# One inverse per right-hand side: the chunked delta rule of a hybrid decoder layer

## The chip, the cores and the metric

The kernel runs on one core of a Trainium2 chip, as one launch. The metric is the device time of the launch in microseconds, the median over the timed runs. The engines are named as in the profile: PE (matmul), PEld (PE's weight loads, which overlap its matmuls), DVE (vector), ACT (scalar), POOL (GpSimd), SP (which issues the weight DMAs).

## What is computed

One decoder layer for 256 prompt tokens and 8 x 8 sample tokens, 320 columns in all: an input projection, three token mixers (RG-LRU, gated delta rule, causal pooling), their gated sum, an output projection and an MLP. The change is in the delta rule, for each of 8 heads:

```
a_mat = eye(C) + where(strict, beta[..., None] * decay * kk, 0.0)
eg = exp(gamma)
rhs = concatenate([beta[..., None] * v, (beta * eg)[..., None] * k], axis=-1)
sol = triangular_solve(a_mat, rhs, lower=True, unit_diagonal=True)
u_c, wk_c = sol[..., :DV], sol[..., DV:]
...
def step(s, inp):
    w = uc - einsum('bhck,bhkv->bhcv', wkc, s)
    o = einsum('bhck,bhkv->bhcv', qg_c, s) + einsum('bhij,bhjv->bhiv', qk_c, w)
    s = gl_c[..., None, None] * s + einsum('bhck,bhcv->bhkv', kd_c, w)
```

With X the inverse of a_mat, w = X (beta v) - X (beta e^gamma k) S, which is also X (beta v - beta e^gamma k S).

## The kernel before

Channels lie on partitions and the 320 tokens on columns. Nearly all work on PE is projections. Their weights stream in tiles of 512 x 256 (512 KB): SP loads a tile into a ring of six (`load`, L251), ACT rounds it to a high part (`split`, L662), DVE makes the low part (`split`, L936), and PE takes the tile in eight blocks of three matmuls, high by high, high by low, low by high (`tile`, L1607; `product`, L1601). PE frees the tile's slot when it is done.

The small work of the mixers is put by hand between these blocks. The delta rule's heads 0 to 3 run under the gated projection of the LRU branch (`gated`, 4 iterations of 12 tiles), heads 4 to 7 under that of the pooling branch. A head is cut into numbered steps k (`dn_step`, one function on each of PE, L1740, DVE, L1295, and ACT, L789; POOL's part is `head`, L482). `dn_place` (L634) says behind which tile and block PE does step k. The first head of each half (0 and 4) is "peeled": its steps lie closer together, since it begins in the middle of an iteration. DVE and ACT do step k some four tiles earlier in their own order of weight tiles (`dn_steps`, L646, and for the peeled heads the lists in `late`), so they stand and wait at each step until PE has come to it, and PE has four tiles in hand meanwhile.

The 256 prompt tokens are two chunks of 128; the 64 sample tokens, eight sequences of eight, are a third. The steps of a head:

- k = 0, 1: rows of decays are spread by PE, DVE scales keys and queries (KT, QT, and KB, the keys by beta), PE forms the products of keys with keys and queries, and turns values and keys over. ACT scales the turned ones into VB (values by beta), KBG (keys by beta and e^gamma) and KDC. POOL masks the decay and forms QG1 and half of WQS, the queries by e^gamma (L490, L491).
- k = 3 to 14: six levels that build XT, the transposed inverse, in PE and DVE by turns.
- k = 15: PE applies the inverse to VB (three products) and to KBG (two: 128 columns of the second chunk and 64 of the samples). ACT copies the five results out of PSUM: W0, U12 (two), the negated samples' half of WQS, and WK1.
- k = 16: PE multiplies W0, does eight narrow products (32 columns of WQS by each sequence's state), and forms the state after the first chunk; ACT copies it (S1), DVE copies the narrow ones (WS).
- k = 17: PE multiplies S1 with WK1 and picks rows of WS; DVE adds both to U12 and spreads the samples (WX).
- k = 18: outputs and new states.

An fp32 product in these steps shows as two matmul rows in the trace (a count of x10 is five products).

Of the kernel before, what the change touches and what calls it, by code (L numbers as in the profile page):

```python
# [6 lines left out]
ALU = mybir.AluOpType  # L7
# [84 lines left out]
def build(nc, A):  # L92
    with ExitStack() as ctx:
# [68 lines left out]
        XT, KT, QT, KB, EG, WK1, QG1, WQS, DTM, LT, QKD = (  # L162
# [3 lines left out]
        VB, KBG, KDC = scr(o, 3 * P), scr(o + 3 * P, 3 * P), scr(o + 6 * P, 3 * P)  # L166
# [29 lines left out]
        def sem(name):  # L196
# [26 lines left out]
         w1_psum, w_ready, fin_psum, dn_done, ss_loaded, ss_stored) = map(sem, (  # L223
# [3 lines left out]
            "dn_done", "dn_state_loaded", "dn_state_stored"))  # L227
# [102 lines left out]
        def _(pool):  # L330
# [151 lines left out]
            def head(h, following):  # L482
# [6 lines left out]
                pool.wait_ge(vt_ready, h + 1)  # L489
                pool.tensor_tensor(QG1, QT[:, P:2 * P], EG[:, P:2 * P], ALU.mult)  # L490
# [13 lines left out]
            def clear_rows():  # L504
# [5 lines left out]
                for t in (VB, KBG):  # L510
                    pool.memset(t[NS:P, 2 * P:3 * P], 0.0)
# [122 lines left out]
        def dn_place(k, peeled):  # L634


            if peeled:
                after = (0, 6, 6, 13, 16, 20, 23, 27, 29, 32, 34, 38, 40, 44, 46, 48, 51, 54, 59)[k]
                return 5 + after // 8, after % 8
# [4 lines left out]
            return (5 + (k - 6) // 2, (3, 7)[k % 2]) if k < 18 else (11, 6)  # L644

        def dn_steps(step, h, late):  # L646

            steps = {}
            for k in (0, 1, *range(3, 19)):
# [7 lines left out]
        def _(act):  # L657
# [131 lines left out]
            def dn_step(h, k):  # L789
# [7 lines left out]
                elif k == 1:  # L797
# [29 lines left out]
            def late(it, t0, h0):  # L827

                if it == 0:
                    return {3: [lambda: gate(0, 1, t0, 0)], 4: [lambda: dn_step(h0, 15), lambda: dn_step(h0, 16)]}  # L830
# [1161 lines left out]
```

## Time and profile before

| | us |
|---|---|
| median of 3 timed runs | 2078.09 (2077.95 to 2078.2) |
| profiled execution, span from first to last instruction | 2076.3 |
| PE busy | 2059.8 (99%) |
| DVE busy | 1205.9 (58%) |
| ACT busy | 775.4 (37%) |
| POOL busy | 215.1 (10%) |
| L1742, most of the delta rule's small products, busy | 83.9 |

The busy times are unions over the whole span, and the engines overlap. Idle time on an engine that is not waited for costs nothing, so the views to read here are the chain that ended last, what the weight loads of PE waited for, and the timeline around the steps.

### The profile page before, as it was taken

The numbers are of one execution on the slowest core, as the hardware profiler recorded it, in microseconds if no ns is written. First come the engines' busy times: TensorE is split into PE (matmuls) and PEld (weight loads), VectorE is DVE, ScalarE is ACT, GpSimd is POOL, SyncE is SP. The second block draws the span as 40 slices with busy tenths as digits, with TensorE's granted clock in tenths as the row PEclk, the third lists the DMA queues.
The fourth block names the chain that finished last, engine by engine and source line by source line (L and its number), as shares of the span: only waits on it lengthen the run. The fifth ranks groups of instructions, "written<-read, shape, count | busy, mean of one in ns | idle before, by whom it ended". The sixth has DMA issues, their size and how long they took to land.

```text
span 2076.3 us, 35424 instructions
## 1 busy us (share of the span) xinstructions
PE 2059.8 (99%) x15117; PEld 2022.1 (97%) x15117; DVE 1205.9 (58%) x2065; ACT 775.4 (37%) x974; POOL 215.1 (10%) x358
## 2 busy tenths in 40 slices
PE   9999999999999999999999999999999999999997
PEld 9999999999999999999999999999999999999997
DVE  7989787566576666655545544444444444444444
ACT  5434555233333233333334433334233333333342
POOL 7322011111241110200001000000000000000001
PEclk9999999999999999999999999999999999999998
DMA  7444454444544444464444445444444445454443
GB/s 245 148 142 142 144 164 124 134 142 136 164 146 130 136 135 132 142 203 151 147 151 152 145 150 153 152 145 150 152 153 145 150 152 153 146 149 152 149 149 108
DMA packets 295644, 309.48 MB, mean 149 GB/s; under 512 B 9713, under 2 KB 290417, under 8 KB 295233
## 3 DMA queue, kind: packets, MB, share of 16 engines
q1 hardware_dynamic: 291616, 291.54, 44.8%
q0 software_dynamic: 3584, 15.55, 2.6%
q8 instruction: 119, 1.95, 0.4%
q14 instruction: 37, 0.30, 0.1%
q10 hardware_dynamic: 288, 0.15, 0.0%
HBM read 298.83 MB, written 8.37 MB: 148 GB/s over the span
## 4 chain that ended last, share of the span: by engine, by line
PE 90%; DVE 6%; issue 1%; POOL 1%; DMA 1%; ACT 1%; SPq 0%; DVEq 0%; ACTq 0%; POOLq 0%
PE main L1603 29%; PE main L1605 28%; PE main L1604 28%; PE aux L1742 3%; DVE lo L940 2%; DVE scratch L947 2%; DVE scratch L940 1%; DMA raw<-in_w_in 1%; DVE scratch L944 0%; PE aux L1854 0%; PE aux L1720 0%; POOL qkv L335 0%; DVE qkv L947 0%; POOL qkv L388 0%; ACT hi L668 0%
## 5 line engine op out<-in xcount | busy, mean ns | idle before, releaser
L940 DVE TENSOR_TENSOR lo<-raw,hi 128x1024 fp32r<-128x1024 f32 x544 | 660.4, 1231 | 342.2 <-ACT hi L668 334.7
L1603 PE MATMUL main<-x_hi,hi 128*128 128x320 f32 x2688 | 839.7, 312 | 1.8 <-DVE x_lo L947 0.8
L1605 PE MATMUL main<-x_hi,lo 128*128 128x320 f32 x2688 | 830.5, 309 | 0.0
L1604 PE MATMUL main<-x_lo,hi 128*128 128x320 f32 x2688 | 830.4, 309 | 0.0
L668 ACT ACTIVATE hi<-raw 128x1024 fp32r<-128x1024 f32 x544 | 564.1, 1054 | 674.8 <-DMA raw<-in_w_up 221.5
L1603 PEld LDWEIGHTS main<-x_hi,hi 128*128 128x128 f32 x2688 | 504.7, 188 | 9.1 <-DVE lo L940 3.8
L1604 PEld LDWEIGHTS main<-x_lo,hi 128*128 128x128 f32 x2688 | 504.8, 188 | 0.7
L1605 PEld LDWEIGHTS main<-x_hi,lo 128*128 128x128 f32 x2688 | 504.5, 188 | 0.0
L1603 PE MATMUL main<-o_hi,hi 128*128 128x320 f32 x1408 | 441.4, 314 | 0.0
L1605 PE MATMUL main<-o_hi,lo 128*128 128x320 f32 x1408 | 435.0, 309 | 0.0
L1604 PE MATMUL main<-o_lo,hi 128*128 128x320 f32 x1408 | 435.0, 309 | 0.0
L1603 PEld LDWEIGHTS main<-o_hi,hi 128*128 128x128 f32 x1408 | 264.4, 188 | 5.8 <-issue 4.6
L1604 PEld LDWEIGHTS main<-o_lo,hi 128*128 128x128 f32 x1408 | 264.5, 188 | 0.0
L1605 PEld LDWEIGHTS main<-o_hi,lo 128*128 128x128 f32 x1408 | 264.3, 188 | 0.0
L940 DVE TENSOR_TENSOR qkv<-main,qkv 128x320 f32<-128x320 f32 x144 | 64.0, 486 | 201.9 <-PE main L1605 201.8
L589 POOL COPY qkv<-gate 128x640 f32<-128x640 f32 x1 | 0.7, 723 | 868.4 <-ACT gate L909 868.4
L1742 PE MATMUL aux<-scratch 32*32 32x32 f32 (+2 forms) x1536 | 83.9, 223 | 0.5 <-DVE scratch L1319 0.4
L1742 PEld LDWEIGHTS aux<-scratch 32*32 32x32 f32 (+2 forms) x1536 | 65.4, 127 | 15.9 <-issue 11.6
L1603 PE MATMUL main<-merged_hi,hi 128*128 128x320 f32 x256 | 79.1, 309 | 0.0
L1604 PE MATMUL main<-merged_lo,hi 128*128 128x320 f32 x256 | 79.1, 309 | 0.0
L1605 PE MATMUL main<-merged_hi,lo 128*128 128x320 f32 x256 | 79.1, 309 | 0.0
L940 DVE TENSOR_TENSOR o_lo<-scratch,o_hi 128x640 fp32r<-128x640 f32 x44 | 36.3, 826 | 59.3 <-ACT o_hi L900 50.4
(283 smaller groups left out, 1212.8 us busy)
## 6 DMA issues: line engine op xcount, KB each, us to landing
raw<-in_w_in SPq DMA_DIRECT2D x210, 512.0 KB, 3.5
raw<-in_w_up SPq DMA_DIRECT2D x128, 512.0 KB, 3.7
raw<-in_w_down SPq DMA_DIRECT2D x128, 512.0 KB, 3.3
raw<-in_w_back SPq DMA_DIRECT2D x80, 512.0 KB, 3.3
scratch<-in_s_in POOLq DMA_DIRECT2D x8, 512.0 KB, 4.9
out_s_out<-scratch POOLq DMA_DIRECT2D x8, 512.0 KB, 4.4
merged<-in_x SPq DMA_DIRECT2D x8, 320.0 KB, 7.6
qkv<-in_x POOLq DMA_DIRECT2D x1, 2560.0 KB, 10.2
```

The lines of the kernel that those rows point to most:

```text
L589: pool.tensor_copy(acc, GS[:]).then_inc(sq2_used, 1)
L668: act.activation(HI[:, slot * TILE:(slot + 1) * TILE], RAW[:, slot * TILE:(slot + 1) * TILE], ACT.Copy).then_inc(hi_ready, 1)
L940: return dve.tensor_tensor(out, a, b, op)
L947: return dve.scalar_tensor_tensor(out=out, in0=a, scalar=s, in1=b, op0=op0, op1=op1)
L1603: pe.matmul(bank, hi, xh, start=first, stop=False)
L1604: pe.matmul(bank, hi, xl, start=False, stop=False)
L1605: return pe.matmul(bank, lo, xh, start=False, stop=last)
L1742: return pe.matmul(out, a, b, start=True, stop=True)
```

## The change

The inverse is applied once, to the right-hand side less the keys' product with the state. POOL forms the scaled keys in the layout of channels on partitions (KG1 and the first half of WQS). KBG is gone. PE takes the state's products first, DVE subtracts them from VB in place, and PE applies the inverse to what is left. Step 15 is now X VB of the first chunk and the narrow products, 16 the state after the first chunk and the rows of WS, 17 the keys by S1 and the inverse for the samples, 18 (new) the inverse for the second chunk, 19 what was 18.

```diff
@@ def build(nc, A):
-        XT, KT, QT, KB, EG, WK1, QG1, WQS, DTM, LT, QKD = (
+        XT, KT, QT, KB, EG, KG1, QG1, WQS, DTM, LT, QKD = (
...
-        VB, KBG, KDC = scr(o, 3 * P), scr(o + 3 * P, 3 * P), scr(o + 6 * P, 3 * P)
+        VB, KDC = scr(o, 3 * P), scr(o + 6 * P, 3 * P)
@@ def head(h, following): and def clear_rows():
                 pool.wait_ge(vt_ready, h + 1)
+                pool.tensor_tensor(KG1, KB[:, P:2 * P], EG[:, P:2 * P], ALU.mult)
+                pool.tensor_tensor(samples_of(WQS, 0), samples_of(KB[:, NP:N], 0), samples_of(EG[:, NP:N], 0), ALU.mult)
                 pool.tensor_tensor(QG1, QT[:, P:2 * P], EG[:, P:2 * P], ALU.mult)
...
-                for t in (VB, KBG):
-                    pool.memset(t[NS:P, 2 * P:3 * P], 0.0)
+                pool.memset(VB[NS:P, 2 * P:3 * P], 0.0)
@@ def dn_place(k, peeled):
             if peeled:
-                after = (0, 6, 6, 13, 16, 20, 23, 27, 29, 32, 34, 38, 40, 44, 46, 48, 51, 54, 59)[k]
+                after = (0, 6, 6, 13, 16, 20, 23, 27, 29, 32, 34, 38, 40, 44, 46, 48, 51, 54, 58, 62)[k]
                 return 5 + after // 8, after % 8
...
-            return (5 + (k - 6) // 2, (3, 7)[k % 2]) if k < 18 else (11, 6)
+            return (5 + (k - 6) // 2, (3, 7)[k % 2])
@@ def _(act): def dn_step(h, k):
-                    for c, n in enumerate((P, P, NS)):
-                        act.activation(KBG[0:n, c * P:(c + 1) * P], AX[3][0:n, c * P:(c + 1) * P], ACT.Copy,
-                                       scale=cols(COL, h, 1, c * 56 + 48, 1, n))
...
                 elif k == 15:
                     act.wait_ge(uw_psum, h + 1)
-                    act.activation(W0, AX[0][:, 0:P], ACT.Copy)
-                    act.activation(U12[:, 0:P], AX[0][:, P:2 * P], ACT.Copy)
-                    act.activation(U12[0:NS, P:2 * P], AX[0][0:NS, 2 * P:3 * P], ACT.Copy)
-                    act.activation(samples_of(WQS, 0), samples_of(AX[1][:, NP:N], 0), ACT.Copy, scale=-1.0)
-                    act.activation(WK1, AX[1][:, P:2 * P], ACT.Copy, scale=-1.0).then_inc(w0_ready, 1)
+                    act.activation(W0, AX[0][:, 0:P], ACT.Copy).then_inc(w0_ready, 1)
                 elif k == 16:
...
+                elif k == 18:
+                    act.wait_ge(u1_psum, h + 1)
+                    act.activation(U12[:, 0:P], AX[2][:, P:2 * P], ACT.Copy).then_inc(u1_ready, 1)
@@ def _(dve): def dn_step(h, k):
+                elif k == 15:
+                    dve.wait_ge(uw_psum, h + 1)
+                    dve.tensor_copy(WS, AX[2][:, 2 * P:3 * P]).then_inc(ws_ready, 1)
                 elif k == 16:
                     dve.wait_ge(s1_psum, h + 1)
-                    dve.wait_ge(s1_ready, h + 1)
-                    dve.tensor_copy(WS, AX[2][:, 2 * P:3 * P]).then_inc(ws_ready, 1)
+                    tt(VB[0:NS, 2 * P:3 * P], VB[0:NS, 2 * P:3 * P], AX[1][0:NS, 2 * P:3 * P], ALU.subtract) \
+                        .then_inc(r2_ready, 1)
                 elif k == 17:
                     dve.wait_ge(w1_psum, h + 1)
-                    tt(U12[:, 0:P], U12[:, 0:P], AX[1][:, P:2 * P], ALU.add)
-                    link(tt(U12[0:NS, P:2 * P], U12[0:NS, P:2 * P], AX[1][0:NS, 2 * P:3 * P], ALU.add))
+                    tt(VB[:, P:2 * P], VB[:, P:2 * P], AX[1][:, P:2 * P], ALU.subtract).then_inc(r1_ready, 1)
+                    link(dve.tensor_copy(U12[0:NS, P:2 * P], AX[0][0:NS, 2 * P:3 * P]))
                     tt(WX.rearrange("p (b v) -> p b v", b=4), U12[0:NS, None, P:2 * P].to_broadcast([NS, 4, P]),
@@ def _(pe): def dn_step(h, k, first):
                 elif k == 15:
                     pe.wait_ge(x_ready, h * 7 + 7)
-                    for c in range(3):
-                        mm(AX[0][:, c * P:(c + 1) * P], wide_x[:, c * P:(c + 1) * P], VB[:, c * P:(c + 1) * P])
-                    for c, lo, hi in ((1, P, 2 * P), (2, NP, N)):
-                        ins = mm(AX[1][:, lo:hi], KBG[:, c * P:(c + 1) * P], XT[:, lo:hi])
+                    pe.wait_ge(qg_ready, h + 1)
+                    pe.wait_ge(ss_loaded, h * 16 + 16)
+                    mm(AX[0][:, 0:P], XT[:, 0:P], VB[:, 0:P])
+                    for r in range(2):
+                        for j in range(4):
+                            b = 2 * j + r
+                            ins = pe.matmul(AX[2][32 * j:32 * (j + 1), 2 * P:3 * P],
+                                            WQS[:, 32 * b - 16 * r:32 * b - 16 * r + 32], SS[:, b * P:(b + 1) * P],
+                                            start=r == 0, stop=r == 1)
                     ins.then_inc(uw_psum, 1)
                 elif k == 16:
                     pe.wait_ge(w0_ready, h + 1)
-                    pe.wait_ge(qg_ready, h + 1)
-                    pe.wait_ge(ss_loaded, h * 16 + 16)
-                    mm(AX[3][:, 0:P], W0, QKD[:, 0:P])
...
-                    mm(AX[2][:, 0:P], KDC[:, 0:P], W0).then_inc(s1_psum, 1)
+                    pe.wait_ge(ws_ready, h + 1)
+                    mm(AX[2][:, 0:P], KDC[:, 0:P], W0)
+                    mm(AX[1][:, 2 * P:3 * P], SELW[:], WS)
+                    mm(AX[3][:, 0:P], W0, QKD[:, 0:P]).then_inc(s1_psum, 1)
                 elif k == 17:
                     pe.wait_ge(s1_ready, h + 1)
-                    pe.wait_ge(ws_ready, h + 1)
-                    mm(AX[1][:, P:2 * P], WK1, S1)
-                    mm(AX[1][:, 2 * P:3 * P], SELW[:], WS).then_inc(w1_psum, 1)
+                    pe.wait_ge(r2_ready, h + 1)
+                    mm(AX[1][:, P:2 * P], KG1, S1)
+                    mm(AX[0][:, 2 * P:3 * P], wide_x[:, 2 * P:3 * P], VB[:, 2 * P:3 * P]).then_inc(w1_psum, 1)
                 elif k == 18:
+                    pe.wait_ge(r1_ready, h + 1)
+                    mm(AX[2][:, P:2 * P], XT[:, P:2 * P], VB[:, P:2 * P]).then_inc(u1_psum, 1)
+                elif k == 19:
                     pe.wait_ge(w_ready, h + 1)
+                    pe.wait_ge(u1_ready, h + 1)
```

The lists for the peeled heads get ACT's step 18 behind the same tile as DVE's step 17, and DVE's step 15 ahead of 16.

PE's instructions around step 15 of head 1, before (L1742 is the small products, aux the PSUM banks they go to, scratch the tiles of the delta rule):

```order
L1605 MATMUL main<-x_hi,lo 128x320
L1742 MATMUL aux<-scratch 128x128 [waits dn_x]
L1742 MATMUL aux<-scratch 128x128 x3
L1742 MATMUL aux<-scratch 128x64
L1603 MATMUL main<-o_hi,hi 128x320 [waits evacuated,lo_ready]
L1604 MATMUL main<-o_lo,hi 128x320
```

and now:

```order
L1606 MATMUL main<-x_hi,lo 128x320
L1743 MATMUL aux<-scratch 128x128 [waits dn_state_loaded,dn_qg,dn_x]
L1798 MATMUL aux<-scratch 32x128 x8
L1604 MATMUL main<-o_hi,hi 128x320 [waits evacuated,lo_ready]
L1605 MATMUL main<-o_lo,hi 128x320
```

Four full products leave step 15 (two of them for good), and the eight narrow ones come in from step 16, with their waits.

DVE's order in the same head, from the last level of the inverse to the copy of the outputs, before:

```order
L940 TENSOR_TENSOR scratch<-scratch,aux 128x256 [waits dn_z_psum]
L940 TENSOR_TENSOR lo<-raw,hi 128x1024 [waits hi_ready]
L1374 COPY scratch<-aux 128x128 [waits dn_s1,dn_s1_psum]
L940 TENSOR_TENSOR gate<-main,rms_scale 128x320 [waits evacuated,tile_used]
L940 TENSOR_TENSOR gate<-main,rms_scale 128x320
L940 TENSOR_TENSOR scratch<-scratch,aux 128x128 [waits dn_w1_psum]
L940 TENSOR_TENSOR scratch<-scratch,aux 64x128
L940 TENSOR_TENSOR scratch<-scratch,batch_mask 64x512 [waits dve_step]
L940 TENSOR_TENSOR lo<-raw,hi 128x1024 [waits hi_ready]
L1383 COPY qkv<-aux 128x320 [waits dn_fin_psum]
```

and now:

```order
L938 TENSOR_TENSOR scratch<-scratch,aux 128x256 [waits dn_z_psum]
L1371 COPY scratch<-aux 128x128 [waits dn_uw_psum]
L938 TENSOR_TENSOR lo<-raw,hi 128x1024 [waits hi_ready]
L938 TENSOR_TENSOR scratch<-scratch,aux 64x128 [waits dn_s1_psum]
L938 TENSOR_TENSOR gate<-main,rms_scale 128x320 [waits evacuated,tile_used]
L938 TENSOR_TENSOR gate<-main,rms_scale 128x320
L938 TENSOR_TENSOR scratch<-scratch,aux 128x128 [waits dn_w1_psum]
L1379 COPY scratch<-aux 64x128
L938 TENSOR_TENSOR scratch<-scratch,batch_mask 64x512 [waits dve_step]
L938 TENSOR_TENSOR lo<-raw,hi 128x1024 [waits hi_ready]
L1384 COPY qkv<-aux 128x320 [waits dn_fin_psum]
```

The copy WS moves ahead of a weight tile's split, the subtraction for the samples stands behind that split, and the one for the chunk behind the gate's two products.

## Rows read from the trace of the kernel before

**Rows 1.** The page's busy times, and one stretch of the view by stretches (PEclk is the last but two)

```profile
PE 2059.8 (99%) x15117; PEld 2022.1 (97%) x15117; DVE 1205.9 (58%) x2065; ACT 775.4 (37%) x974; POOL 215.1 (10%) x358
...
373.00:428.00 55.00, 55.00 (x516) 51.92 (x515) 33.68 (x83) 18.00 (x32) 7.84 (x11) 1.00 0.45 134
```

**Rows 2.** The page's chain that ended last, by line

```profile
PE main L1603 29%; PE main L1605 28%; PE main L1604 28%; PE aux L1742 3%; DVE lo L940 2%; DVE scratch L947 2%; DVE scratch L940 1%; DMA raw<-in_w_in 1%; DVE scratch L944 0%; PE aux L1854 0%; PE aux L1720 0%; POOL qkv L335 0%; DVE qkv L947 0%; POOL qkv L388 0%; ACT hi L668 0%
```

**Rows 3.** Waits of PE's weight loads: 326 to 368 us, 605 to 660, 660 to 820

```profile
PEld aux L1742 <- DVE scratch L940: 0.5, 2, 0.3
PEld aux L1742 <- DVE scratch L1319: 0.3, 1, 0.3
...
PEld aux L1742 <- DVE scratch L1319: 0.7, 1, 0.7
PEld aux L1742 <- DVE scratch L1353: 0.3, 1, 0.3
...
PEld aux L1742 <- DVE scratch L940: 0.6, 3, 0.2
```

**Rows 4.** Timeline of PE, head 1, steps 15 to 18 (start, duration, engine, line)

```profile
408.99 0.31 PE L1605 MATMUL main<-x_hi,lo 128*128 128x320 f32 x1
409.14 1.22 PE L1742 MATMUL aux<-scratch 128*128 128x128 f32 x10
...
410.40 0.31 PE L1604 MATMUL main<-o_lo,hi 128*128 128x320 f32 x1
...
411.87 0.31 PE L1605 MATMUL main<-o_hi,lo 128*128 128x320 f32 x1
...
413.38 0.31 PE L1604 MATMUL main<-o_lo,hi 128*128 128x320 f32 x1
...
414.85 0.31 PE L1605 MATMUL main<-o_hi,lo 128*128 128x320 f32 x1
...
415.59 0.31 PE L1604 MATMUL main<-o_lo,hi 128*128 128x320 f32 x1
...
418.96 0.33 PE L1816 MATMUL aux<-scratch 128*128 128x64 f32 x2
419.13 0.39 PE L1817 MATMUL aux<-ident,scratch 128*128 128x64 f32 x2
```

**Rows 5.** Timeline of ACT and DVE, head 1, steps 15 to 17

```profile
410.40 0.28 ACT L811 ACTIVATE scratch<-aux 128x128 f32<-128x128 f32 x1 [9.13 <-PE aux L1742]
...
411.15 1.06 ACT L668 ACTIVATE hi<-raw 128x1024 fp32r<-128x1024 f32 x1
...
412.25 1.23 DVE L940 TENSOR_TENSOR lo<-raw,hi 128x1024 fp32r<-128x1024 f32 x1 [4.24 <-ACT hi L668]
...
414.02 0.88 DVE L940 TENSOR_TENSOR gate<-main,rms_scale 128x320 f32<-128x320 f32 x2
415.64 0.48 DVE L940 TENSOR_TENSOR scratch<-scratch,aux 128x128 f32<-128x128 f32 x2 [0.74 <-PE aux L1742]
416.15 0.68 DVE L940 TENSOR_TENSOR scratch<-scratch,batch_mask 64x512 f32<-64x512 f32 x1
```

**Rows 6.** Timeline of DVE, head 0, steps 15 and 18

```profile
358.62 1.23 DVE L940 TENSOR_TENSOR lo<-raw,hi 128x1024 fp32r<-128x1024 f32 x1 [1.04 <-ACT hi L668]
...
368.24 2.40 DVE L947 SCALAR_TENSOR_TENSOR scratch<-scratch,aux 128x128 f32<-128x128 f32 x9
```

**Rows 7.** Timeline of POOL in head 0, DVE and PE in head 1, steps 1 and 3

```profile
331.67 1.44 POOL L490 TENSOR_TENSOR scratch<-scratch 128x128 f32<-128x128 f32 x1
333.08 1.30 POOL L491 TENSOR_TENSOR scratch<-scratch 128x64 f32<-128x64 f32 x1
...
376.90 1.53 DVE L940 TENSOR_TENSOR lo<-raw,hi 128x1024 fp32r<-128x1024 f32 x1 [0.91 <-ACT hi L668]
...
381.08 0.16 DVE L1319 STREAM_TRANSPOSE scratch<-scratch 64x32 f32<-64x32 f32 x1
...
383.45 0.38 PE L1742 MATMUL aux<-scratch 32*32 32x32 f32 x20
```

More of the change, by code:

```diff
@@ L226, in build @@
             "dn_z_psum", "dn_uw_psum", "dn_w0", "dn_s1_psum", "dn_s1", "dn_ws", "dn_w1_psum", "dn_w", "dn_fin_psum",
-            "dn_done", "dn_state_loaded", "dn_state_stored"))
+            "dn_done", "dn_state_loaded", "dn_state_stored", "dn_rhs_samples", "dn_rhs", "dn_u1_psum", "dn_u1"))
         pool_loaded, pfx_ready, ptail_copied, d_ready, py_psum = map(sem, (
@@ L643, in dn_place @@
                 return (5 + (k - 6) // 2, (2, 6)[k % 2])
-            return (5 + (k - 6) // 2, (3, 7)[k % 2]) if k < 18 else (11, 6)
+            return (5 + (k - 6) // 2, (3, 7)[k % 2])
         def dn_steps(step, h, late):
             steps = {}
-            for k in (0, 1, *range(3, 19)):
+            for k in (0, 1, *range(3, 20)):
                 pos = dn_place(k, False)[0] + 4
@@ L829, in late @@
                 if it == 0:
-                    return {3: [lambda: gate(0, 1, t0, 0)], 4: [lambda: dn_step(h0, 15), lambda: dn_step(h0, 16)]}
+                    return {3: [lambda: gate(0, 1, t0, 0)], 4: [lambda: dn_step(h0, 15), lambda: dn_step(h0, 16)],
+                            5: [lambda: dn_step(h0, 18)]}
                 steps = dn_steps(dn_step, it + h0, True)
@@ L1393, in gated @@
                 gate0, merge0 = lambda: gate(n0, t0, it, 0), lambda: merge(n0, t0, g0, it, 0, branch)
-                dn = [lambda k=k: dn_step(h0, k) for k in range(19)]
+                dn = [lambda k=k: dn_step(h0, k) for k in range(20)]
                 own = {8: [gate0], 10: [merge0]}
@@ L1404, in late @@
                 gate1, merge1 = lambda: gate(n0, t0, it, 1), lambda: merge(n0, t0, g0, it, 1, branch)
-                dn = [lambda k=k: dn_step(h0, k) for k in range(19)]
+                dn = [lambda k=k: dn_step(h0, k) for k in range(20)]
                 if h0 is not None and it == 0:
                     return {1: [dn[7], dn[8]], 2: [dn[9], dn[10], dn[11]], 3: [dn[12], gate1, dn[13], dn[14]],
-                            4: [dn[16]], 5: [dn[17], merge1, dn[18]]}
+                            4: [dn[15], dn[16]], 5: [dn[17], merge1, dn[19]]}
                 if h0 is None:
@@ L1797, in dn_step @@
                     pe.wait_ge(w0_ready, h + 1)
-                    pe.wait_ge(qg_ready, h + 1)
-                    pe.wait_ge(ss_loaded, h * 16 + 16)
-                    mm(AX[3][:, 0:P], W0, QKD[:, 0:P])
-                    for r in range(2):
-                        for j in range(4):
-                            b = 2 * j + r
-                            pe.matmul(AX[2][32 * j:32 * (j + 1), 2 * P:3 * P], WQS[:, 32 * b - 16 * r:32 * b - 16 * r + 32],
-                                      SS[:, b * P:(b + 1) * P], start=r == 0, stop=r == 1)
-                    mm(AX[2][:, 0:P], KDC[:, 0:P], W0).then_inc(s1_psum, 1)
+                    pe.wait_ge(ws_ready, h + 1)
+                    mm(AX[2][:, 0:P], KDC[:, 0:P], W0)
+                    mm(AX[1][:, 2 * P:3 * P], SELW[:], WS)
+                    mm(AX[3][:, 0:P], W0, QKD[:, 0:P]).then_inc(s1_psum, 1)
                 elif k == 17:
                     pe.wait_ge(s1_ready, h + 1)
-                    pe.wait_ge(ws_ready, h + 1)
-                    mm(AX[1][:, P:2 * P], WK1, S1)
-                    mm(AX[1][:, 2 * P:3 * P], SELW[:], WS).then_inc(w1_psum, 1)
+                    pe.wait_ge(r2_ready, h + 1)
+                    mm(AX[1][:, P:2 * P], KG1, S1)
+                    mm(AX[0][:, 2 * P:3 * P], wide_x[:, 2 * P:3 * P], VB[:, 2 * P:3 * P]).then_inc(w1_psum, 1)
                 elif k == 18:
+                    pe.wait_ge(r1_ready, h + 1)
+                    mm(AX[2][:, P:2 * P], XT[:, P:2 * P], VB[:, P:2 * P]).then_inc(u1_psum, 1)
+                elif k == 19:
                     pe.wait_ge(w_ready, h + 1)
+                    pe.wait_ge(u1_ready, h + 1)
                     pe.matmul(AX[3][:, P:2 * P], S1, QG1, start=True, stop=False)
@@ L1827, in gated @@
                     for h in (h0, it + h0) if it == 1 else (it + h0,):
-                        for k in (0, 1, *range(3, 19)):
+                        for k in (0, 1, *range(3, 20)):
                             j, b = dn_place(k, h == h0)
```

3 lines of the change are left out of this document (1 added, 2 removed).

## The prediction

> **What bounds the kernel now.** I read the page first for the busiest engine. PE is busy 99% of the span, and in the stretch from 373 to 428 us, which holds one whole head of the delta rule, PE is busy 55.00 of 55.00 us at a granted clock of 1.00 [rows 1]: the upper level, 2.4 GHz. The chain of waits says the same: 85% of it are the three lines of the large products and 3% is L1742, the small products of the delta rule [rows 2]. Last I read what PE's weight loads waited for. From 660 to 820 us (heads 5 to 7) there are three waits on DVE, 0.6 us together; head 4 has single waits of 0.7 and 0.3 us, head 0 has 0.5 and 0.3 [rows 3]. So what a head does on PE is paid in full, and what it does on DVE, ACT and POOL costs nothing until PE reaches a step whose input is not there. I therefore count PE's instructions, and then look for each new input whether it is in time.
>
> **The unit prices on PE** are in the timeline of head 1 [rows 4]. A large product starts 0.147 us after the one before it (from 410.40 to 411.87, ten of them). The cost of a step between two large ones is the time from the last large product before it to the second behind it, less two such pitches (the second, because the first is also stretched):
> - two products of 128 columns: 415.59 - 414.85 - 0.294 = 0.446 us, 0.223 each;
> - step 15, four of 128 columns and one of 64: 410.40 - 408.99 - 0.294 = 1.116 us, five times 0.223. The 64 columns cost as much as 128;
> - step 16, two of 128 and the eight narrow ones with the states: 413.38 - 411.87 - 0.294 = 1.216 us.
> A step as such has no price of its own here: five products in one step cost what they would in two.
>
> **The sum on PE, per head.** Removed: both products of the scaled keys with the inverse, one of 128 and one of 64 columns, 2 x 0.223 = 0.446 us. All others stay and are only dealt out otherwise: the eight narrow ones move from step 16 to 15, W0's with QKD goes behind two others in 16, the samples' product with the inverse moves from 15 to 17, that of the second chunk to the new step 18. Before: 1.116 + 1.216 + 0.446 = 2.778 us. Now: step 15 is 1.216 - 0.223 = 0.993, step 16 is 0.669, 17 is 0.446, 18 is 0.223, together 2.331. The difference is again 0.446 us, and 8 heads make **3.57 us**. The bounds: inside step 19 (old 18) a product of 64 columns is followed after 0.17 us [rows 4]. With 0.17 for the short one the sum is 8 x 0.39 = 3.1 us. I take 0.223, since in step 15 itself, where the product is removed, it cost that. The upper bound is 3.57 plus waits that PE has now.
>
> Each of these products is two matmul rows, so a row's pitch is 0.111 us. The Trainium skill (TensorE: Matmul & The Clock Gate, Back-to-back issue gap) gives about 81 ns for a matmul of 128 columns in a stream with its weight loads. By it the four rows that go are worth at most 8 x 4 x 0.081 = 2.6 us. The trace's pitch is a third above that figure, and the sum goes by the trace.
>
> **What leaves and joins the other engines.** ACT loses three scalings at step 1 and four of five copies at step 15, and gains one copy at step 18. POOL gains two products per head, ahead of the two it has. DVE gains one small copy of 64 rows and a step 15 that waits for PE. None of this is on the path by itself; what counts is when PE's inputs come. POOL's memset that goes is hidden as it was.
>
> **New waits of PE, middle heads** [rows 5]. Steps 15 to 19 now lie four blocks apart, 12 x 0.147 = 1.76 us.
> - Step 15 ends at about 410.1. ACT's copy W0 takes 0.28, and DVE's copy WS of the same size I take as equal: both there at 410.5; PE asks at 411.9.
> - Behind W0 ACT splits a weight tile (1.06 us) and DVE follows (1.23): 410.5 + 1.06 + 1.23 = 412.8. Only then does DVE subtract the samples (0.25): 413.1. PE asks in step 17 at 414.3. Behind these two on DVE wait the gate's two products (0.88 together), done at about 414.
> - Step 17's result is there at 414.9; the subtraction of the chunk takes 0.25, so 415.2; PE asks in step 18 at 416.5. The copy and the 0.68 us product behind it end at 416.2.
> - Step 18's result is copied by ACT by 417.1; PE asks at 418.5.
> The least slack is 1.2 us. Step 19 stays within a block of where it was, and DVE's long update behind it with it.
>
> **New waits, heads 0 and 4** [rows 6]. Here the spacing is three blocks, 1.32 us, from 15 to 17. In head 0 DVE's split of 358.62 ends at 359.85, and WS is copied behind it: 360.15. PE wants it at 360.0: **0.2 us of waiting**. For the chunk's subtraction the chain is S1's copy until 361.5, ACT's split until 362.6, DVE's split of 1.23 until 363.8, the subtraction until 364.05; PE asks for it at 364.4, slack 0.35. Step 19 comes 1.0 us later than step 18 did, and the next head's first products wait for DVE's update behind it (the nine operations of 2.40 us, ended at 370.64 before): ready at about 371.8, asked for at 372.9. That is what is late next, if anything is.
>
> **The forecast**: 3.57 - 0.2 = 3.4 us less. On the profiled execution, 2076.3 to 2072.9 us of span. The timed runs have a median of 2078.09, 1.8 us above this span for what lies outside it; I take that as unchanged: 2078.09 - 3.4 = **2074.7 us**. 0.2% is 4.16 us, about what a measurement here can tell from no change, so this lies within it, if not by much (0.16%).
>
> **The rivals.**
> - **POOL holds DVE back at step 1.** The two new products come before the query's, so POOL reads SBUF for longer while DVE builds the blocks whose inverse PE waits for in step 3. Their prices are those of the two that exist, 1.44 and up to 1.30 us [rows 7]. In head 1 the blocks are ready at 381.24 and PE comes at 383.45: 2.2 us of cover against 1.44 + 0.32. In heads 0 and 4 PE waits at that step already [rows 3], so there any delay is paid: at most 2.74 + 1.76 = 4.5 us, giving 2074.7 + 4.5 = 2079.2 us; half of it 2077. Against it: most of DVE's step 1 already runs beside work of POOL. The Trainium skill (SBUF — State Buffer, SBUF: two separate sides) has it that a DVE operation with two SBUF inputs and a GpSimd operation exclude each other for the whole instruction; by that rule this rival would be the outcome. No row here shows a full block: DVE's split takes 1.53 us beside POOL's product [rows 7] and 1.23 alone [rows 5].
> - **The round trip that was added is too long: slower.** Step 17's subtraction stands on DVE behind a split, which needs a tile from DMA and ACT. Were that tile late in every head, PE would wait in step 17 or 18. It decides from 3.4 + 4.16 = 7.6 us, 0.95 us in each of 8 heads, that is an input 2.2 us later than worked out above for the middle heads. With 3 us the waiting is 1.8 us a head: 2074.7 + 14 = 2089 us. Against it: the tile that ACT splits at 411.15 needed no wait of its own, its idle time lies before the copy of 410.40.
> - **The waits that PE has now shrink too: faster.** ACT is free about 0.8 us sooner at step 1 (three operations of 0.28) and 0.5 sooner at step 15 (from 410.40 to 411.15, less one copy). If half of the 1.8 us of rows 3 that PE waits in heads 0 and 4 went, 3.57 + 0.9 gives 2073.6 us. Against it: those waits are on DVE's own results [rows 3], which ACT doesn't feed.
> - **The short product costs less than a full one.** Then the removal is worth 3.1 us, by the 0.17 us of rows 4, and the time is 2075.2 us.
>
> **Chances.** Forecast as told 0.75; POOL's hold 0.10; waits shrink 0.08; the short product 0.04; round trip 0.03. Faster by over 0.2% (under 2073.9): the third with a little of the forecast's spread, 0.11. Slower (over 2082.2): round trip and a rest of POOL's hold, 0.04. Within: 0.85. The range takes in the forecast's bounds (3.1 to 4.4 us) and half of POOL's hold: 2073.7 to 2077.2.
>
> **What would show it.** Right: 30 matmul rows a head in steps 15 to 18 instead of 34, 16 of them the narrow ones; those steps cost 2.33 us by the same reading; PE's waits on DVE grow by 0.2 in head 0 alone; ACT's nine scalings become six. Wrong: a new wait of PE on DVE's subtraction or ACT's U12 copy in heads 1 to 3 and 5 to 7; a longer wait at step 3 with POOL's products beside it (POOL's hold); a pitch other than 0.22 us for plain products, or a price for leaving the narrow ones towards a large product that no row of step 16 has, where a plain product follows them.

## The result and the profile after

The change makes the kernel slower. The median of 11 runs is 2083.03 us (2081.24 to 2085.28) against 2078.03 us for the kernel before on the same chip (2077.41 to 2078.95); the ratio is 1.0024, 95% interval 1.0017 to 1.0032. The forecast was 2074.7 us. The profiled execution has a span of 2081.1 us against 2076.3: 4.8 us more. One of the eleven runs of pool_twice below had a mean granted clock of 0.849 and took 2216.06 us; it is in the range given there and not in the ratio.

The page of the changed kernel, and its chain that ended last by line. Against [rows 1] PE has 32 matmul rows fewer (15085 for 15117), ACT 48 instructions fewer, POOL 14 and DVE 8 more; one entry of the chain has no counterpart in [rows 2], `DMA out_p_out<-scratch`, the store of the prompt's state:

```profile
PE 2059.1 (99%) x15085; PEld 2020.7 (97%) x15085; DVE 1208.4 (58%) x2073; ACT 766.3 (37%) x926; POOL 218.6 (11%) x372
...
PE main L1604 28%; PE main L1606 27%; PE main L1605 27%; PE aux L1743 3%; DVE lo L938 2%; DVE scratch L945 2%; DVE scratch L938 2%; DMA raw<-in_w_in 1%; DMA out_p_out<-scratch 1%; DVE scratch L942 0%; PE aux L1859 0%; PE aux L1721 0%; POOL qkv L335 0%; DVE qkv L945 0%; ACT hi L669 0%
```

The removed products are gone at the price that was forecast. The timeline of PE in head 1, steps 15 and 16, read as [rows 4] were (last large product before the step, second one behind it, less 0.294 us):

```profile
412.83 0.31 PE L1606 MATMUL main<-x_hi,lo 128*128 128x320 f32 x1
412.98 0.38 PE L1743 MATMUL aux<-scratch 128*128 128x128 f32 x2
413.30 0.64 PE L1798 MATMUL aux<-scratch 128*32 128x128 f32 x16
414.12 0.31 PE L1605 MATMUL main<-o_lo,hi 128*128 128x320 f32 x1
...
415.59 0.31 PE L1606 MATMUL main<-o_hi,lo 128*128 128x320 f32 x1
...
416.55 0.31 PE L1605 MATMUL main<-o_lo,hi 128*128 128x320 f32 x1
```

414.12 - 412.83 - 0.294 = 0.996 us, then 0.666, and read the same way 0.436 and 0.226 for steps 17 and 18: 2.32 us, where the steps cost 2.778 before and 2.331 were forecast. In no head does PE wait at step 17, 18 or 19.

The loss lies elsewhere. The waits of PE's weight loads in the changed kernel, from 368 to 422 us (head 1); the same rows with the same numbers stand from 660 to 715 us (head 5). Columns are total us, number, and us of the longest:

```profile
PEld aux L1743 <- DVE scratch L938: 2.1, 1, 2.1
...
PEld aux L1743 <- DVE scratch L1317: 0.8, 1, 0.8
```

L938 is step 4 and L1317 step 3. Before, head 5 had no wait over 0.2 us [rows 3]. And behind the second of these waits, in both heads, TensorE's granted clock falls to its lower level. Stretches of the view by stretches, the changed kernel (busy us and count of PE, PEld, DVE, ACT and POOL, then PEclk, share and GB/s of DMA):

```profile
384.00:387.90 3.90, 2.06 (x49) 1.75 (x49) 3.60 (x8) 0.50 (x1) 0.01 (x1) 1.00 0.39 125
387.90:391.30 3.40, 3.40 (x45) 2.96 (x33) 0.72 (x5) 2.13 (x3) 0.00 (x0) 0.52 0.02 5
391.30:395.00 3.70, 3.70 (x41) 3.28 (x41) 2.10 (x7) 0.94 (x1) 0.00 (x0) 0.98 0.43 142
677.90:681.50 3.60, 3.60 (x34) 3.21 (x33) 1.59 (x5) 1.42 (x2) 0.00 (x0) 0.53 0.27 91
```

For 3.4 us from 387.9 and 3.6 us from 677.9 the granted clock is 0.52 and 0.53 of 2.4 GHz: 1.2 GHz for nearly all of it. The kernel before has 1.00 in the same stretches. So PE did 3.40 x 0.48 = 1.6 us less work there than its busy time tells, and "PE busy 99%" shows nothing of it.

**Where 4.8 us come from.** The first small product of a head (step 0, four rows of `aux<-head_rows`) marks its start. Timeline of PE, the kernel before, then the changed one:

```profile
373.09 0.75 PE L1742 MATMUL aux<-head_rows,row_pickers 128*128 128x320 f32 x4
...
428.37 0.60 PE L1742 MATMUL aux<-head_rows,row_pickers 128*128 128x320 f32 x3
...
660.24 0.75 PE L1742 MATMUL aux<-head_rows,row_pickers 128*128 128x320 f32 x4
...
715.51 0.75 PE L1742 MATMUL aux<-head_rows,row_pickers 128*128 128x320 f32 x4
```

```profile
372.94 0.75 PE L1743 MATMUL aux<-head_rows,row_pickers 128*128 128x320 f32 x4
...
431.75 0.75 PE L1743 MATMUL aux<-head_rows,row_pickers 128*128 128x320 f32 x4
...
662.20 0.75 PE L1743 MATMUL aux<-head_rows,row_pickers 128*128 128x320 f32 x4
...
721.07 0.75 PE L1743 MATMUL aux<-head_rows,row_pickers 128*128 128x320 f32 x4
```

Head 1 took 428.37 - 373.09 = 55.28 us and takes 58.81, 3.53 more. Head 5 took 55.27 and takes 58.87, 3.60 more. These two make +7.13 us. All the rest is 2.3 us shorter: six heads save 0.45 each, 2.7 us, and by the same reading of the steps small waits give back 1.1 of it (0.7 at step 4 in heads 2, 6 and 7; 0.7 in head 0, of which 0.5 at step 10; less 0.3 that head 4 no longer waits). The 0.7 us that remain lie outside the steps of the delta rule. Within head 1 the sum closes: +3.53 and the 0.45 that was saved make 3.98. Steps 3, 4 and 5 cost 1.13, 2.58 and 0.96 us by the reading of [rows 4], where each cost 0.50 before: 3.17 of it. The other 0.8 lies in large products at the lower clock. By cause it is 1.6 us of clock and 2.4 us of waiting.

### The profile page after: what moved, and what is told of

It is laid out like the page before. It is cut to its first block, busy times and chain, and to the rows that moved or that the text cites. A ratio compares the mean times of both kernels' runs of the same rounds, so it can differ in the third digit from the quotient of the medians.

```text
span 2081.1 us, 35342 instructions
## 1 busy us (share of the span) xinstructions
PE 2059.1 (99%) x15085; PEld 2020.7 (97%) x15085; DVE 1208.4 (58%) x2073; ACT 766.3 (37%) x926; POOL 218.6 (11%) x372
## 4 chain that ended last, share of the span: by engine, by line
PE 87%; DVE 8%; DMA 2%; issue 1%; POOL 1%; ACT 1%; SPq 0%; DVEq 0%; ACTq 0%; POOLq 0%
PE main L1604 28%; PE main L1606 27%; PE main L1605 27%; PE aux L1743 3%; DVE lo L938 2%; DVE scratch L945 2%; DVE scratch L938 2%; DMA raw<-in_w_in 1%; DMA out_p_out<-scratch 1%; DVE scratch L942 0%; PE aux L1859 0%; PE aux L1721 0%; POOL qkv L335 0%; DVE qkv L945 0%; ACT hi L669 0%
## 5 line engine op out<-in xcount | busy, mean ns | idle before, releaser
L938 DVE TENSOR_TENSOR lo<-raw,hi 128x1024 fp32r<-128x1024 f32 x544 | 659.5, 1229 | 319.9 <-ACT hi L669 312.5
L938 DVE TENSOR_TENSOR qkv<-main,qkv 128x320 f32<-128x320 f32 x144 | 64.1, 486 | 202.8 <-PE main L1606 202.7
L938 DVE TENSOR_TENSOR o_lo<-scratch,o_hi 128x640 fp32r<-128x640 f32 x44 | 36.3, 825 | 59.3 <-ACT o_hi L898 50.4
```

Of the source, the lines that this page charges most:

```text
L938: return dve.tensor_tensor(out, a, b, op)
```

## How 1.2 us became 2.4

The chain does not run through PE. Timeline of POOL between heads 0 and 1, the kernel before: store of the samples' states, of the prompt's state (not shown), the load of the next head's states behind both, the masking of the decay behind the load's issue, and the first product behind the mask (start, duration; in brackets the idle time before and its releaser):

```profile
370.94 0.95 POOL L496 DMA_DIRECT2D out_s_out<-scratch  x1 [34.42 <-DVE scratch L947]
...
375.52 0.90 POOL L484 DMA_DIRECT2D scratch<-in_s_in  x1 [2.49 <-DMA out_p_out<-scratch]
376.44 0.88 POOL L487 TENSOR_TENSOR scratch<-scratch,mask_incl 128x320 f32<-128x320 f32 x1
377.27 1.48 POOL L490 TENSOR_TENSOR scratch<-scratch 128x128 f32<-128x128 f32 x1
```

The same of the changed kernel:

```profile
372.10 0.95 POOL L498 DMA_DIRECT2D out_s_out<-scratch  x1 [35.21 <-DVE scratch L945]
...
378.60 0.90 POOL L484 DMA_DIRECT2D scratch<-in_s_in  x1 [4.41 <-DMA out_p_out<-scratch]
379.52 0.89 POOL L487 TENSOR_TENSOR scratch<-scratch,mask_incl 128x320 f32<-128x320 f32 x1
380.36 0.47 POOL L490 TENSOR_TENSOR scratch<-scratch 128x128 f32<-128x128 f32 x1
```

The last step's update ends on DVE at 371.80 (its row is below), 1.16 us later than before, and the stores start 372.10 - 370.94 = 1.16 us later. They also take longer: from the first store to the release of the load it was 4.6 us and is 6.5. SP begins to issue the four weight tiles of this stretch at 369.76 before and at 369.62 now, so the later stores may fall behind more of the tiles' traffic, which no run separates; the 64 KB store lands 3.3 us after its issue before, and 5.3 now. The mask starts 3.08 us later. DVE, the changed kernel, head 0's last step and head 1's steps 1 to 4:

```profile
369.40 2.40 DVE L945 SCALAR_TENSOR_TENSOR scratch<-scratch,aux 128x128 f32<-128x128 f32 x9
...
376.75 1.23 DVE L938 TENSOR_TENSOR lo<-raw,hi 128x1024 fp32r<-128x1024 f32 x1 [0.92 <-ACT hi L669]
380.51 0.55 DVE L938 TENSOR_TENSOR scratch<-aux,scratch 128x256 f32<-128x256 f32 x2 [2.54 <-POOL scratch L487]
381.10 1.76 DVE L938 TENSOR_TENSOR scratch<-scratch,block_masks 32x96 f32<-32x96 f32 x4
...
383.70 0.16 DVE L1317 STREAM_TRANSPOSE scratch<-scratch 64x32 f32<-64x32 f32 x1
...
384.23 2.34 DVE L938 TENSOR_TENSOR lo<-raw,hi 128x1024 fp32r<-128x1024 f32 x2
386.49 0.87 DVE L938 TENSOR_TENSOR gate<-main,rms_scale 128x320 f32<-128x320 f32 x2
387.29 0.30 DVE L938 TENSOR_TENSOR scratch<-aux,block_masks 128x64 f32<-128x64 f32 x2
```

The masked decay is what DVE's two operations of 128x256 need. Before, they started at 378.36 without a wait, behind the split of [rows 7], and the mask, done at 377.32, was 1.0 us early. Now DVE stands idle for 2.54 us. Everything behind is in order on DVE: the blocks, two splits (2.34 us), the gate's products (0.87), and only then step 3's result, at 387.29. In the kernel before, those two operations, step 3's result and the PE row of step 4 that needs it are

```profile
378.36 0.54 DVE L940 TENSOR_TENSOR scratch<-aux,scratch 128x256 f32<-128x256 f32 x2
...
384.73 0.30 DVE L940 TENSOR_TENSOR scratch<-aux,block_masks 128x64 f32<-128x64 f32 x2
...
385.27 0.38 PE L1742 MATMUL aux<-scratch 32*32 32x32 f32 x20
```

with 385.27 - 385.03 = 0.24 us of cover. So: mask 3.08 us later, less 1.0 (its own cover on DVE), less 0.24, plus 0.45 of DVE operations that last longer beside POOL (1.76 for 1.46 us, 0.60 for 0.45), plus 0.15 by which PE is ahead, gives 2.4 us of waiting, which is what was found above for the share of the waits; the view of the waits has 2.9 us in its two pieces.

## The experiments

Each kernel was timed in five rounds against the kernel before, and beside each median stand the range and the number of runs. The kernel before had medians of 2077.91 us (late_step, place59, mask_first, no_products), 2078.05 (pool_twice, place59_pool_last, mask_first_pool_last, place61) and 2077.97 (late_mask_first, before_mask_first, both_orders_place59).

**late_step: the kernel before with its last step as late as the changed one's.**

```diff
-                after = (..., 48, 51, 54, 59)[k]
+                after = (..., 48, 51, 54, 62)[k]
```

> The kernel before with one number changed: in heads 0 and 4 the last step (outputs and states) comes three blocks later, as in the change. No product, copy or wait differs. If the loss comes from this placement (the states are finished later, POOL's stores and the mask of the next head's decay behind them, and DVE's step 1 behind that): PE waits 2.5 to 3.5 us at steps 3 to 5 of heads 1 and 5, the granted clock falls once behind each of these waits, and the time is 2083 to 2088 us. If the loss comes from the new products of POOL or from the added round trip: 2078 us, as before.

2084.24 us (2081.68 to 2085.73, 9), ratio 1.0028 (1.0018 to 1.0038). One number in a table, with every product of before in its place, costs 6.3 us, as much as the whole change within the noise (5.0). POOL, then waits of PE's weight loads from 368 to 426 us, of this kernel:

```profile
371.82 0.95 POOL L496 DMA_DIRECT2D out_s_out<-scratch  x1 [35.79 <-DVE scratch L947]
...
378.52 0.90 POOL L484 DMA_DIRECT2D scratch<-in_s_in  x1 [4.61 <-DMA out_p_out<-scratch]
379.44 0.89 POOL L487 TENSOR_TENSOR scratch<-scratch,mask_incl 128x320 f32<-128x320 f32 x1
```

```profile
PEld aux L1742 <- DVE scratch L940: 2.1, 1, 2.1
...
PEld aux L1742 <- DVE scratch L1319: 0.5, 1, 0.5
```

The stores take 6.7 us, and the granted clock falls likewise (0.60 from 388 to 392 us). Neither POOL's new products nor the new step is needed for the loss.

**no_products: the kernel before without the two products that the change removes.**

```diff
                     for c in range(3):
-                        mm(AX[0][...], wide_x[...], VB[...])
-                    for c, lo, hi in ((1, P, 2 * P), (2, NP, N)):
-                        ins = mm(AX[1][:, lo:hi], KBG[...], XT[:, lo:hi])
+                        ins = mm(AX[0][...], wide_x[...], VB[...])
```

> The kernel before without the two products of the scaled keys with the inverse in step 15 (ACT copies what the banks hold, so the samples' and the second chunk's results are not those of the reference); nothing else differs. It prices what the change removes. If a row of either costs PE 0.111 us, as the sum had it: 3.6 us less, 2074.5 us. If the short one costs less: 3.1 us less, 2074.9 us. By the 81 ns of the rule: 2.6 us less, 2075.4 us.

2074.85 us (2073.65 to 2075.94, 11), ratio 0.9985 (0.9976 to 0.9994): 3.06 us less (1.2 to 5.0 by the interval), where 3.6 were expected. Step 15 costs 0.67 us for 1.12, so the product of 64 columns cost as much as the one of 128. In the profile each undisturbed head's delta steps sum to 12.66 us against 13.11, the 0.45 of the forecast; in head 4 PE waits 0.35 us longer than before at step 13, which is most of the difference in that execution.

**place59: the change with its last step where the last step was before.**

```diff
-                after = (..., 51, 54, 58, 62)[k]
+                after = (..., 51, 54, 57, 59)[k]
```

> The change with two numbers altered: in heads 0 and 4 step 18 comes one block and step 19 three blocks earlier, where the last step stood before. If the placement is the cause: no waits at steps 3 to 5 of heads 1 and 5, no fall of the clock, perhaps 0.1 to 0.5 us of waiting at steps 18 and 19 of heads 0 and 4, and 2074.5 to 2076 us. If POOL's products are: the waits stay and the time is 2081 to 2083 us.

2077.57 us (2076.6 to 2078.91, 11), ratio 0.9998 (0.9989 to 1.0007). Better than the change by 5.5 us, but 1.6 us above what was expected. PE still waits 1.1 us at step 4 in head 1 and 0.9 in head 5 by the view of the waits (the step costs 0.96 and 0.67 us more than 0.50); the clock stays at 1.00. The stores took 5.0 us, the mask was 0.57 us later than before, and DVE's split beside it was more than twice as long. Timeline of DVE and POOL:

```profile
377.12 2.96 DVE L938 TENSOR_TENSOR lo<-raw,hi 128x1024 fp32r<-128x1024 f32 x1 [0.92 <-ACT hi L669]
...
377.01 0.87 POOL L487 TENSOR_TENSOR scratch<-scratch,mask_incl 128x320 f32<-128x320 f32 x1
377.83 0.47 POOL L490 TENSOR_TENSOR scratch<-scratch 128x128 f32<-128x128 f32 x1
378.25 0.32 POOL L491 TENSOR_TENSOR scratch<-scratch 128x64 f32<-128x64 f32 x1
378.53 0.45 POOL L492 TENSOR_TENSOR scratch<-scratch 128x128 f32<-128x128 f32 x1
378.95 1.31 POOL L493 TENSOR_TENSOR scratch<-scratch 128x64 f32<-128x64 f32 x1
```

**place61: the change with its last step one block earlier.** The only edit is 62 to 61 in the same line.

> The change with step 19 of heads 0 and 4 one block earlier (0.44 us). If the waits of heads 1 and 5 grow with the lateness of the last step one for one: they are 0.4 to 0.5 us a head shorter than in the change at step 3, and little shorter at step 4 if the granted clock still falls. If it still falls twice: 2081.5 to 2082.5 us. If it doesn't fall any more: 2078 to 2079.5 us.

2077.77 us (2076.32 to 2081.55, 11), ratio 1.0001 (0.9992 to 1.001). Waits from 368 to 426 us, and stretches around the place where the clock fell in the changed kernel:

```profile
PEld aux L1743 <- DVE scratch L938: 1.5, 1, 1.5
```

```profile
387.90:391.30 3.40, 3.40 (x58) 2.95 (x57) 2.18 (x7) 0.74 (x1) 0.00 (x0) 1.00 0.46 154
...
680.00:684.00 4.00, 4.00 (x47) 3.71 (x40) 3.44 (x7) 0.19 (x2) 0.00 (x0) 1.00 0.39 131
```

A wait of 1.5 us (1.7 in head 5), all of it at step 4, and no fall. The stores took 4.75 us here, not 6.5. By the cost of steps 3 and 4 over 0.50 us each, head 1 loses 0.96, 1.34 and 2.70 us with the last step at block 59, 61 and 62. So the last block, 0.44 us, is worth 1.4 us in these steps of head 1 and 1.1 in head 5, far more than the one for one that was expected, since the stores get slower with it. Between the two profiled executions (2076.3 and 2081.1 us) the clock takes another 3.2 us, and place61 for its part waits 0.9 us more at step 13 of head 4 (the step costs 1.33 us for 0.45): 2.5 and 3.2 less 0.9 are the 4.8 us. One of the eleven timed runs of place61 took 2081.55 us, 2.6 more than any other; it was not profiled, so it isn't known whether the clock fell in it.

**mask_first: the change with the mask ahead of the load that waits for the stores.** POOL's order within a head is now mask, wait for the stores, load.

```diff
-                pool.dma_start(SS..., A["s_in"]...).then_inc(ss_loaded, 16)
                 pool.wait_ge(dt_exp, h + 1)
                 pool.tensor_tensor(DTM, DTM, MASKI[:], ALU.mult).then_inc(dtm_ready, 1)
+                if isinstance(h, int) and h:
+                    pool.wait_ge(ss_stored, h * 32)
+                pool.dma_start(SS..., A["s_in"]...).then_inc(ss_loaded, 16)
...
-                pool.wait_ge(ss_stored, h * 32 + 32)
+                if not following:
+                    pool.wait_ge(ss_stored, h * 32 + 32)
```

> The change with its placement as it is, but POOL masks the decay of the next head before it waits for the stores of the states, and only then loads the next states. If the chain is stores, then mask, then DVE's step 1: the waits of heads 1 and 5 go though the last step is as late as in the change, and the time is 2074 to 2076 us. If DVE's step 1 is late by itself: 2081 to 2083 us.

2074.96 us (2074.34 to 2076.49, 11), ratio 0.9986 (0.9977 to 0.9995): 3.0 us less than before and 8.1 less than the change, with all steps where the change has them. POOL:

```profile
374.77 0.88 POOL L485 TENSOR_TENSOR scratch<-scratch,mask_incl 128x320 f32<-128x320 f32 x1 [0.98 <-ACT scratch L798]
...
378.09 0.94 POOL L488 DMA_DIRECT2D scratch<-in_s_in  x1 [2.44 <-DMA out_p_out<-scratch]
```

The load is as late as in the changed kernel (the stores took 6.4 us here too), but the mask waits for ACT's exponential alone and starts at 374.77 instead of 379.52. PE's longest wait in head 1 is 0.3 us.

**late_mask_first and before_mask_first: the same order of POOL in late_step and in the kernel before.**

> late_step (the kernel before with the last step of heads 0 and 4 three blocks later) with POOL's mask ahead of its wait for the stores. If the late last step costs only through stores and mask: the 6 us of late_step are gone, 2077.5 to 2078.5 us, and no clock falls. If it costs through DVE's update or anything else as well: 2080 us or more.

> The kernel before with only POOL's order changed (mask ahead of the wait for the stores). If the mask is never late in it: 2078 us, within 0.5. Then mask_first is worth something in the change alone, and what the change then gives is what the two products cost. If the mask is what PE's short waits in the kernel before come from: 2077 us or less.

2078.33 us (2076.89 to 2078.83, 11), ratio 1.0000 (0.9991 to 1.001), and 2078.06 us (2077.21 to 2078.45, 11), ratio 0.9999 (0.999 to 1.0008). The order takes back 5.9 of the 6.3 us that late_step costs, and is worth nothing that can be measured where the last step was early enough. That is the chain through the stores and the mask, shown from both sides. In mask_first the gain is therefore the removal's own, but for one step: head 4's step 3 costs 0.99 us before and 0.51 to 0.68 in the five kernels with this order.

**pool_twice: the kernel before with two more of POOL's products ahead of its own.**

```diff
+                ch.link(pool.tensor_tensor(QG1, ...))
+                ch.link(pool.tensor_tensor(samples_of(WQS, DT), ...))
                 pool.tensor_tensor(QG1, ...)
```

> The kernel before, in which POOL forms its two products of step 1 twice in every head, each of the first two followed by a wait of POOL for itself. No PE work and no placement differs. If POOL's reads hold DVE back while it builds the blocks of step 1: PE waits 0.2 to 0.9 us at step 4 of the heads 1 to 3 and 5 to 7, and the time is 2079 to 2081 us. If POOL's products are harmless: 2078 us and no such waits.

2078.46 us (2077.45 to 2216.06, 11), ratio 1.0001 (0.9992 to 1.001). No new wait in heads 1 to 3 and 5 to 7, and 0.1 us at step 3 of head 4. But this doesn't clear the changed kernel's products. Here each of the two added products is followed by POOL's wait for itself, and DVE can start in between: in head 2 the first ends at 432.78 us, the next starts at 432.86, and DVE's split beside them takes 1.50 us. In head 2 of the changed kernel two products stand in front of the split with no gap, and it takes 2.00 us. DVE and the last of its step 1:

```profile
435.57 2.00 DVE L938 TENSOR_TENSOR lo<-raw,hi 128x1024 fp32r<-128x1024 f32 x1 [0.92 <-ACT hi L669]
...
440.21 0.16 DVE L1317 STREAM_TRANSPOSE scratch<-scratch 64x32 f32<-64x32 f32 x1
```

From the head's start to the end of that transpose it is 8.62 us, and 8.03 before. Read so in heads 1 to 3 and 5 to 7 of all kernels of this text, step 4 costs 0.50 us as long as this time is under some 8.40 us, and above that more by the excess: 0.74 us at 8.62, 1.17 at 9.06, 1.84 at 9.73. (In heads 1 and 5 of the changed kernel and late_step, at 10.5 to 11.0 us, steps 3 and 4 share the excess and the lower clock adds to it; late_mask_first alone has 0.1 us more at 8.0.) The kernel before has 7.5 to 8.3 us, and pool_twice 7.8 to 8.4.

**place59_pool_last: place59 with all four products behind the next head's rows.**

```diff
+                if following:
+                    rows(h + 1).then_inc(rm_ready, 1)
                 pool.tensor_tensor(KG1, ...)
...
-                if following:
-                    rows(h + 1).then_inc(rm_ready, 1)
```

> The change with the last step of heads 0 and 4 where it was before (as in place59), and POOL's four products behind its rows for the next head instead of ahead of them, so that they lie beside DVE's weight tiles rather than beside its step 1. If POOL's hold is what is left in place59: its waits at step 4 (0.95 and 0.67 us in heads 1 and 5, 0.14 to 0.29 in 2, 6 and 7) shrink to under 0.2 us each, and the time is 2075 to 2076 us. If they come from elsewhere: 2077.5 us, as place59.

2076.03 us (2075.47 to 2077.66, 11), ratio 0.9992 (0.9983 to 1.0001). The waits at step 4 of heads 1 and 5 fall from 1.1 and 0.9 us to 0.4 and 0.5 (the step's cost from 1.46 and 1.17 to 0.71 and 0.83, so not to under 0.2 in head 5), and DVE's split from 2.96 us to 1.60:

```profile
376.44 1.60 DVE L938 TENSOR_TENSOR lo<-raw,hi 128x1024 fp32r<-128x1024 f32 x1 [0.91 <-ACT hi L669]
```

So the products do cost something, and this order gives back about 1.5 us of the 1.6 that place59 missed. Up to 0.3 us of head 1's share may not be theirs: in this execution the stores took 4.67 us for 4.95, and the mask stood 0.26 us earlier in the head. In heads 2 and 6, whose mask is in time in both kernels, the waits at step 4 go (0.78 and 0.79 us to 0.51) and DVE's step 1 ends at 8.35 us; in head 7, where no head follows and the order is therefore the old one, the wait stays (0.67). So the hold does not need a late mask; a late mask makes it dearer.

**mask_first_pool_last and both_orders_place59: the edits together.** The first is mask_first with that order of the products, the second has the table of place59 as well.

> The change with both edits of POOL's order: the mask ahead of the wait for the stores, and the four products behind the rows. The placement is that of the change. Under the theory of chain and hold together: no waits at steps 3 to 5 beyond those of the kernel before, and 2074.0 to 2074.8 us. If moving the products makes them late for step 15, PE waits there and the time is above 2075.

> The change with POOL's mask first, POOL's products last, and the last step of heads 0 and 4 where it was before. mask_first_pool_last already has all but the last. If the last step's place no longer matters once the mask is off the chain: 2074.8 us, within 0.5. If it matters still: under 2074.3.

2074.84 us (2073.62 to 2076.72, 11), ratio 0.9986 (0.9977 to 0.9995), and 2075.48 us (2074.59 to 2076.17, 11), ratio 0.9988 (0.9979 to 0.9997). The second is 0.7 us above what was expected. In both, heads 2 and 6 still wait 0.2 us at step 4: the rows for the next head now stand where the products stood, and DVE's step 1 ends as late (8.60 us). With the mask first neither the products' place nor the last step's is worth anything that can be measured. The version that beats both kernels is the change with the mask first: 3 us below the kernel before.

## Why the prediction was wrong

**The sum on PE: right.** 3.57 us were forecast, no_products and mask_first show 3.1 and 3.0 (each within 1 to 5 by its interval), and the steps read 0.996, 0.666, 0.436 and 0.226 us against 0.993, 0.669, 0.446 and 0.223. The pitch of 0.111 us a row held, and for the short product too, so that rival is out. The Trainium skill (TensorE: Matmul & The Clock Gate, Back-to-back issue gap) gives about 81 ns, by which the removal would be worth 2.6 us; by the rows of the steps the trace decides for 0.111, though the timed 3.1 us lies as near to the one as to the other.

**New waits, middle heads: right for steps 15 to 19.** PE waits at none of them. What is new there is 0.2 us at step 4 in heads 2, 6 and 7. It is POOL's work beside DVE's step 1, the mechanism of the rival, in small: that step ends 8.58 to 8.64 us behind these heads' start, 7.95 to 8.06 before, and what lies over 8.40 is waited for. Six of the seven kernels with the change's four products show it in heads 2 and 6 (0.1 to 0.3 us); place59_pool_last doesn't. Of those with two products or pool_twice's spaced four only no_products has any, 0.1 us in head 2, where the mask came 0.5 us later than before.

**New waits, heads 0 and 4: here it failed.** 0.2 us of waiting in head 0 was right (step 16 costs 0.93 us in place of 0.67). Also right, within 0.05 us, was the next sentence: "Step 19 comes 1.0 us later than step 18 did, and the next head's first products wait for DVE's update behind it: ready at about 371.8, asked for at 372.9." The update is done at 371.80, and PE's step 0 starts at 372.94 without a wait. The step that failed is the one after it, "That is what is late next, if anything is": only PE was followed from that update. A second engine waits for it. POOL stores the states when the update is done, waits for both stores, issues the next head's load and only then masks the decay, and the mask is an input of DVE's step 1. The two transfers in between were in no term of the forecast. What the runs show in place of that step: the update 1.16 us later, the mask 3.08 us later, and behind it 2.4 us of waiting and 1.6 us of lower clock in each of heads 1 and 5, 8.0 us together. That outweighs the 3.57 us that the eight heads save.

**The cover was taken at the wrong place.** The rival of POOL's hold had 2.2 us of cover at step 3 (blocks ready at 381.24, PE at 383.45). DVE's order has two splits and the gate between the blocks and step 3's result, and there the cover is 0.24 us, at step 4; with the mask's 1.0 us before DVE it is 1.28. The 1.16 us by which the stores start later would have used up all but 0.1 of it even had the stores taken no longer.

**The rivals.** POOL's hold: its mechanism was real and its place wrong. It costs 0.7 us at step 4 of heads 2, 6 and 7, where the forecast saw cover enough, 1.5 us by the timed runs where the mask is late as well (place59_pool_last), and nothing at step 3 of heads 0 and 4, for which up to 4.5 us were priced (0.51 and 0.90 us, 0.58 and 0.99 before). For the Trainium skill's rule (SBUF — State Buffer, SBUF: two separate sides), that a DVE operation with two SBUF inputs and a GpSimd operation exclude each other for the whole instruction, the forecast said that no row showed a full block. Runs made since do. POOL's product takes 0.47 us by itself and 1.48 beside DVE's split, and in place61 the mask takes 1.86 in place of 0.89, each 1.0 us more: it is waiting for DVE to end. In place59 the split takes 2.96 in place of 1.23, 1.73 more, nearly the 1.86 us from its start at 377.12 to the end of POOL's third product at 378.98. The rule and the trace agree, and the 1.44 us that the forecast took for a product was 0.47 of work and the rest waiting. Even so, the rule did not bring the rival's outcome: the exclusion costs only what DVE's slack does not cover, which before the change was 0.25 us in head 1 and 0.34 to 0.45 in heads 2, 6 and 7.

The round trip that was added had the right sign with the wrong place: no wait at steps 17 or 18. That waits would shrink: head 4's did by 0.3 us, head 0's grew. The fall of the clock was in no case of the forecast, and by itself it is 3.2 of the 7.1 us that heads 1 and 5 lost.

**What stays open.** PE waits 1.1 us at step 13 of head 4 in mask_first (0.2 before, none in the changed kernel, 0.6 in no_products), and head 0's step 10 varies from kernel to kernel in the same way (0.05 to 1.0 us, the most in before_mask_first). Each kernel has one trace, so whether the timed runs have these waits, and whether they are what separates mask_first's 3.0 us from the 3.57 of the sum, isn't known; their cause was not tried. That the fall of the clock comes from the two waits is read from their order in time; no run has the one without the other. That the stores take longer because they meet the weight tiles is argued from the times of both; no run moved the tiles.

## What to carry to other kernels

When a step ends later, list every engine that waits for its last semaphore, and follow each of them, through the transfers it waits for, to the next instruction that the busy engine needs; the one that it meets first need not be the one that is late. Measure the cover at the last instruction of the queue before the busy engine, not at the first product of the chain. And don't let an instruction that others need stand in a queue behind a wait that it does not need itself: putting the mask ahead of the load turned a loss of 5.0 us into a gain of 3.0.

## What the hardware did that was not expected

- Behind two waits of PE one step apart, 0.8 and 2.1 us in the changed kernel and 0.5 and 2.1 us in late_step, the granted clock was at the lower level for some 3.4 us, in heads 1 and 5 of both. Behind waits of 1.5 and 1.7 us in place61 and 1.1 us in place59 it stayed at 1.00. A fall costs about 1.6 us, two thirds of what the waiting before it cost, and PE's busy share does not show it.
- The two stores on POOL's queue (512 and 64 KB) held the next load for two durations and nothing between: 4.6 to 5.0 us where the first store was issued 1.2 to 2.1 us behind SP's first weight tile of the stretch (before, no_products, pool_twice, place59, place59_pool_last, place61), and 6.4 to 6.7 us where it was 2.5 to 2.6 us behind it (mask_first, mask_first_pool_last, late_step, late_mask_first, the changed kernel), in heads 1 and 5 alike. In before_mask_first and both_orders_place59 the stores had landed before the mask in front of the load was done, and their time can't be read.
